# First loads reordered, the gate bias added by VectorE from a broadcast row, and the rotated key turned two tiles later

## The chip, the cores and the metric

The kernel runs on one core of one Trainium2 chip. The metric is the device time of one execution in microseconds, lower is better. Before the change three runs gave 3794.58, 3788.32 and 3795.59 us, median 3794.58 us.

## The reference, cut to what matters

Two transformer blocks run one after the other on 256 tokens of width 2048, all in float32. The change lies in the first block, ahead of its expert layer:

```python
h = rmsnorm(x, g_norm1[l])
proj = h @ w_in[l]
c_q = proj[..., :OFF_CQ]
c_kv = proj[..., OFF_CQ:OFF_CKV]
k_pe = proj[..., OFF_CKV:OFF_KPE]
z_sgu = proj[..., OFF_KPE:OFF_SGU]
gates = jax.nn.sigmoid(proj[..., OFF_SGU:] + b_gate[l])
o_a = mla_branch(c_q, c_kv, k_pe, positions, ...)   # attention; k_pe is rotated (rope) and shared by all heads
o_b = sgu_branch(z_sgu, ...)
merged = gates[..., :D_MODEL] * o_a + gates[..., D_MODEL:] * o_b
x = x + merged @ w_out[l]
```

After it come a product-key expert layer with 16384 experts (the longest part of the program), a second block with attention, a state-space scan and a gated feed-forward, which the change does not touch.

## The kernel before, in words

**Weight tiles.** Every weight matrix comes as a stream of numbered tiles of 128 partitions x 1024 float32 (512 KB). SyncE loads them into `raw`, a ring of 8, in program order. ScalarE rounds a tile to `hi` (the helper `split` of ScalarE, line 662), VectorE takes the rest, `lo = raw - hi` (line 1216), and TensorE multiplies in three passes, `xh*hi`, `xh*lo` and `xl*hi` (lines 2143 to 2145, 12 matmuls of 512 columns a tile). `hi` and `lo` are rings of 4, so ScalarE splits tile n+4 when TensorE is through with tile n. The split of n+4 stands in ScalarE's and VectorE's programs in the turn of tile n, and everything else that these engines do stands between two splits, in an order written out by hand. All waits are on semaphores.

**Start.** SyncE issues the four parts of `X` (2 MB), then eight weight tiles. GpSimd issues the constants `const`, the columns `cols`, the positions and the spatial weights `wsp`, in this order. TensorE turns `X` by transposes (`turn`, line 2176), two 128-column pieces a round, eight rounds ("h1"), of which the first two come before the first tile and the others behind tiles 0 to 5. ScalarE makes `xh` of a round (line 691), VectorE `xl` (lines 1256, 1258), and tile j needs round j. The first transpose waits for both `const` and `cols` (`small_in` at 32) and for half of `X`. The row norms of `X` come from two squares with a row sum on ScalarE (line 676), VectorE and GpSimd make the inverse root of them. The norm of a row is a factor 1/r that is multiplied in when a result leaves PSUM.

**Chunks.** A chunk is eight tiles, 512 output columns for 256 tokens, in one of two pairs of PSUM banks (`ab`), which ScalarE empties (`evac`, line 702) and gives back by `acc_free`. The order is: c_q, c_kv, the 64 columns of the key part `kpe`, then four rounds r = 0 to 3 of a gate chunk of `gm` and eight tiles of the attention's projections (parts 0 to 3 of two tiles each) for four heads, then `zv`, `zu`, the four gate chunks of `gb`, `out` and `pq`. The attention of round r-1 (`scores`, `probsT`, `values` on TensorE, `soft_in`, `soft_out` on VectorE, `probs` on ScalarE) is spread over the tiles of round r.

**Gate bias.** The result in PSUM must be r times the bias larger than the product, since the factor 1/r follows. So `gate_chunk` starts with two plain float32 matmuls of one row: the row of r (`srow`, turned by two matmuls at line 2198) times the row of the bias (`brow`, line 2278). The trace has 4 MATMUL records for the two. ScalarE's sigmoid then reads PSUM with scale 1/r and gives the banks back.

**Rotated key.** `kpe` is rotated on VectorE (`rope32`, lines 1312 to 1317) into `KPR` behind the split of tile 12 of round 0 (8 gate tiles, then 4 on), and TensorE turns it at line 2326 behind tile 9 of the round (part 0, second tile). Two memsets of `KP2` (line 1407) come before the turn is let through.

Of the kernel before, what the change touches and what calls it, by code (L numbers as in the profile page):

```python
# [12 lines left out]
ALU = mybir.AluOpType  # L13
# [4 lines left out]
P = 128  # L18
S, TT = 256, 2
D, KD = 2048, 16  # L20
CH = 512
# [23 lines left out]
ROOT1, ROOT2, STD1 = 152, 156, 160  # L45
# [55 lines left out]
MOD_TILES = (0, 4)  # L101
LNSUM = 228
# [28 lines left out]
def build(nc, A, out):  # L131
    V, SC, PE_, GP = nc.vector, nc.scalar, nc.tensor, nc.gpsimd
    ctx = ExitStack()
    with ctx:
# [37 lines left out]
        brow = at("brow", [1, 2 * CH], W0 + 73)  # L172
# [13 lines left out]
        srow = at("srow", [1, S], W0 + 85)  # L186
# [62 lines left out]
        neghalf = at("neghalf", [P, 32], W0 + 84.5)  # L249
# [65 lines left out]
        x_in = [sem(f"x_in{t}") for t in range(TT)]  # L315
        small_in, pos_in = sem("small_in"), sem("pos_in")
# [6 lines left out]
        bias_in, bias_used = [sem(f"bias_in{b}") for b in range(2)], sem("bias_used")  # L323
        kpe_T, kpe_ps, kpe_out = sem("kpe_T"), sem("kpe_ps"), sem("kpe_out")
# [3 lines left out]
        kpr_ok, row_ps, row_ok = sem("kpr_ok"), sem("row_ps"), sem("row_ok")  # L328
# [16 lines left out]
        mod2_in, mod2_used, mod2_ps = sem("mod2_in"), sem("mod2_used"), sem("mod2_ps")  # L345
# [18 lines left out]
        br_out, mod2_ok = sem("br_out"), sem("mod2_ok")  # L364
# [23 lines left out]
        def _(sp):  # L388
# [16 lines left out]
            for half in range(2):  # L405
                for t in range(TT):
                    h = slice(half * D // 2, (half + 1) * D // 2)
                    sp.dma_start(X[:, t, h], A["x"][:, t, h]).then_inc(x_in[half], 16)

            def bias(i):  # L410
                if i >= 2:
                    sp.wait_ge(bias_used, i - 1)
                sp.dma_start(brow[:, CH * (i % 2):CH * (i % 2) + CH], A["b_gate"][i:i + 1, :]).then_inc(bias_in[i % 2], 16)

            for j in range(2 * TC):
                load(A["w_in"][j], j)
# [13 lines left out]
            for j in range(8 * TC):  # L430
                load(A["w_in"][6 * TC + j], BASE["zv"] + j)
            for c in range(4):
                bias(4 + c)
                for j in range(TC):
                    load(A["w_in"][(14 + c) * TC + j], BASE["gb"] + c * TC + j)
# [49 lines left out]
        def _(pool):  # L485
            pool.dma_start(const[:], A["const"]).then_inc(small_in, 16)
            pool.dma_start(cols[:], A["cols"]).then_inc(small_in, 16)
            pool.dma_start(posi[:], A["pos"]).then_inc(pos_in, 16)
            pool.dma_start(wsp[:], A["w_spatial"]).then_inc(pos_in, 16)
            GP.memset(neghalf[:], -0.5).then_inc(pow_ok, 1)  # L490
            count = [0]
# [12 lines left out]
            pool.wait_ge(small_in, 32)  # L504
# [147 lines left out]
        def _(act):  # L652
# [51 lines left out]
            act.wait_ge(small_in, 32)  # L704
# [14 lines left out]
            act.wait_ge(trig_arg, 2)  # L719
# [3 lines left out]
            act.wait_ge(row_ps, 1)  # L723
            SC.copy(srow[:], ps[0:1, 6, 0:S]).then_inc(row_ok, 1)
            split(BASE["kpe"] + SPL)
            act.wait_ge(tile_used, BASE["kpe"] + 1)
            SC.copy(KPT[0:ROPE], ps[0:ROPE, 4, 0:S]).then_inc(kpe_T, 1)
# [29 lines left out]
            for r in range(4):  # L757
                n0, use = BASE["gm"] + (TC + 4 * TL) * r, 2 + 5 * r
                for j in range(TC):
# [9 lines left out]
                    elif j == 1:  # L769
                        act.wait_ge(kpe_ps, 1)  # L770
                        for u in range(TT):
                            SC.activation(KPE[:, u], ps[:, 5, u * ROPE:(u + 1) * ROPE], ACT.Copy,
                                          scale=stat[:, ROOT1 + 2 + u:ROOT1 + 3 + u]).then_inc(kpe_out, 1)
# [4 lines left out]
                if r == 0:  # L778
                    act.wait_ge(trig_arg, 2)
                    act.wait_ge(trig_ok, 1)  # L780
                evac(n0 + TC, use % 2, lambda t: GM[:, t, CH * r:CH * r + CH], ACT.Sigmoid, ROOT1)
                n0 += TC
                for j in range(4 * TL):
# [3 lines left out]
                    if r == 0 and j == 2:  # L787
                        act.wait_ge(row_ps, 2)
                        for b in range(2):
                            rows = slice(ROPE * b, ROPE * b + ROPE)  # L790
                            SC.copy(KP2[rows, b], ps[rows, 6, 0:S]).then_inc(row_ok, 1)
# [43 lines left out]
            for c in range(4):  # L835
# [4 lines left out]
                if c == 0:  # L840
                    act.wait_ge(ln_done, 2)
                if c >= 2:
                    act.wait_ge(merged_ok, c - 1)
                evac(BASE["gb"] + (c + 1) * TC, c % 2, lambda t: GB[:, c % 2, t], ACT.Sigmoid, ROOT1)

            def mod2_load(u):
                act.wait_ge(mod2_used, u)
                if u == 0:
                    act.wait_ge(bias_used, 8)
# [358 lines left out]
        def _(dve):  # L1208
# [53 lines left out]
            dve.wait_ge(small_in, 32)  # L1262
# [3 lines left out]
            mean_sq(2, D, 2, ROOT1)  # L1266
            for j in range(TC, TC + SPL):
                split(j)
            dve.wait_ge(rstd_ready, 1)
            V.tensor_tensor(stat[:, STD1:STD1 + 2], stat[:, ROOT1:ROOT1 + 2], stat[:, ROOT1 + 2:ROOT1 + 4], ALU.mult  # L1270
                            ).then_inc(trig_arg, 1)

            dve.wait_ge(pos_in, 32)
# [17 lines left out]
            splits(TC, TC)  # L1291

# [76 lines left out]

            split(BASE["kpe"] + SPL)  # L1370
            for r in range(4):
                n0, use = BASE["gm"] + (TC + 4 * TL) * r, 2 + 5 * r
                for j in range(TC):
# [18 lines left out]
                    if r == 1 and j in (2, 5):  # L1392
                        coefficients(j // 3)
                n0 += TC
                for j in range(4 * TL):
# [3 lines left out]
                    if r == 0 and j == 0:  # L1399
                        dve.wait_ge(kpe_out, 2)  # L1400
# [56 lines left out]
            def merge(c):  # L1457

                dve.wait_ge(acc_free[c % 2], 2 * (PB["gb"] + c // 2 + 1))
# [1401 lines left out]
```

## Time and profile before

| | |
|---|---|
| median of three runs | 3794.58 us |
| the profiled execution, its own time | 3794.6 us |
| its span, first to last instruction | 3793.0 us |
| TensorE busy | 3677.6 us, 97% |
| VectorE busy | 2672.0 us, 70% |
| ScalarE busy | 1781.7 us, 47% |
| GpSimd busy | 143.0 us, 4% |
| mean granted TensorE clock | 0.983 |
| first block up to the start of `out` | about the first 585 us |

The profile's page gives the busy time of each engine and the chain of work that ended last. A timeline lists instructions in order: start, duration, engine, line, output and inputs, and in brackets how long the engine sat idle before and who ended it. In a timeline overlapping instructions are common, the start of the next is what counts. The view of stretches gives for each the busy time of TensorE, the granted clock as a share of 2.4 GHz (1.00 or 0.50), the share in which the DMA engines were busy, and GB/s.

### The profile page before, as it was taken

How to read it: one execution, taken by the hardware profiler on the slowest of the kernel's cores; microseconds unless marked ns; L12 is line 12 of the kernel's file. 1: busy time of each engine (PE TensorE's matmuls, PEld its weight loads, DVE VectorE, ACT ScalarE, POOL GpSimd, SP SyncE). 2: the span in 40 equal slices, each digit the busy share in tenths (PEclk: the TensorE clock that was granted, in tenths of full speed). 3: DMA queues.
4: the chain of work that ended last, by engine and by line, in shares of the span. 5: the costliest groups of instructions: out<-in, count | busy, mean ns of one | idle time of the engine just before them, and what ended most of it. 6: DMA issues, size and time to landing. Idle time of an engine off the chain costs nothing.

```text
span 3793.0 us, 49880 instructions
## 1 busy us (share of the span) xinstructions
PE 3677.6 (97%) x17366; PEld 3064.2 (81%) x17366; DVE 2672.0 (70%) x3500; ACT 1781.7 (47%) x2127; POOL 143.0 (4%) x208
## 2 busy tenths in 40 slices
PE   8999999999899999999999997999999899999998
PEld 6888878888788888888888886877788688888886
DVE  4555547668797878777778886788876646666567
ACT  4554444444454444443434444556654444545553
POOL 3000000000000000000000000010000000000000
PEclk9999999999999999999999998999999899999999
DMA  6445557857558988888877874554446455555663
GB/s 220 150 145 191 186 161 271 280 176 222 178 217 307 353 296 322 296 322 298 312 266 277 282 264 153 178 162 156 157 156 197 142 169 186 189 187 184 193 186 124
DMA packets 208607, 825.92 MB, mean 218 GB/s; under 512 B 23640, under 2 KB 24152, under 8 KB 194880
## 3 DMA queue, kind: packets, MB, share of 16 engines
q1 hardware_dynamic: 175840, 638.15, 50.9%
q10 hardware_dynamic: 14400, 102.77, 7.2%
q0 software_dynamic: 18208, 82.84, 5.9%
q8 instruction: 105, 1.72, 0.2%
q14 instruction: 54, 0.44, 0.0%
HBM read 785.39 MB, written 38.27 MB: 217 GB/s over the span
## 4 chain that ended last, share of the span: by engine, by line
PE 91%; DVE 4%; ACT 3%; issue 2%; DMA 0%; POOL 0%; SPq 0%; ACTq 0%; DVEq 0%
PE ps L2143 27%; PE ps L2145 27%; PE ps L2144 27%; PE ps L2450 2%; ACT hi L662 1%; DVE lo L1216 1%; PE ps L2222 1%; PE ps L2223 1%; PE ps L2224 1%; PE ps L2583 1%; PE ps L2476 1%; PE ps L2571 1%; PE ps L2176 1%; PE ps L2237 1%; PE ps L2687 0%
## 5 line engine op out<-in xcount | busy, mean ns | idle before, releaser
L1216 DVE TENSOR_TENSOR lo<-raw,hi 128x1024 fp32r<-128x1024 f32 (+1 forms) x1217 | 1479.5, 1219 | 1013.5 <-ACT hi L662 1010.6
L662 ACT CAST hi<-raw 128x1024 fp32r<-128x1024 f32 (+1 forms) x1217 | 1274.4, 1048 | 1864.8 <-PE ps L2145 1813.7
L2143 PE MATMUL ps<-hi,xh 128*128 128x512 f32 x2880 | 1145.6, 398 | 11.0 <-DVE lo L1216 7.1
L2145 PE MATMUL ps<-hi,xl 128*128 128x512 f32 x2880 | 1128.2, 392 | 0.0
L2144 PE MATMUL ps<-lo,xh 128*128 128x512 f32 x2880 | 1127.7, 392 | 0.0
L2143 PEld LDWEIGHTS ps<-hi,xh 128*128 128x128 f32 x2880 | 545.1, 189 | 130.7 <-issue 11.6
L2145 PEld LDWEIGHTS ps<-hi,xl 128*128 128x128 f32 x2880 | 544.6, 189 | 115.7
L2144 PEld LDWEIGHTS ps<-lo,xh 128*128 128x128 f32 x2880 | 545.1, 189 | 110.5
L2143 PE MATMUL ps<-hi,Ph 128*128 128x512 f32 x1024 | 401.9, 392 | 0.0
L2145 PE MATMUL ps<-hi,Pl 128*128 128x512 f32 x1024 | 399.4, 390 | 0.0
L2144 PE MATMUL ps<-lo,Ph 128*128 128x512 f32 x1024 | 399.1, 390 | 0.0
L2145 PEld LDWEIGHTS ps<-hi,Pl 128*128 128x128 f32 x1024 | 192.6, 188 | 40.4
L2143 PEld LDWEIGHTS ps<-hi,Ph 128*128 128x128 f32 x1024 | 192.7, 188 | 39.3 <-DVE X L1670 0.2
L2144 PEld LDWEIGHTS ps<-lo,Ph 128*128 128x128 f32 x1024 | 192.7, 188 | 39.0
L1670 DVE TENSOR_TENSOR X<-X,ps 128x512 f32<-128x512 f32 x256 | 163.4, 680 | 0.0
L2143 PE MATMUL ps<-hi,Fh 128*128 128x512 f32 x352 | 140.0, 398 | 6.6 <-DVE Y L2068 5.9
L1643 DVE SCALAR_TENSOR_TENSOR macc<-mraw,stat,macc 128x2048 f32<-128x2048 f32 x60 | 140.7, 2345 | 1.4 <-DMA mraw<-in_w_mod 1.4
L2145 PE MATMUL ps<-hi,Fl 128*128 128x512 f32 x352 | 137.9, 392 | 0.0
L2144 PE MATMUL ps<-lo,Fh 128*128 128x512 f32 x352 | 137.6, 391 | 0.0
L2143 PEld LDWEIGHTS ps<-hi,Fh 128*128 128x128 f32 x352 | 66.5, 189 | 21.3 <-DVE Y L2068 7.1
L2145 PEld LDWEIGHTS ps<-hi,Fl 128*128 128x128 f32 x352 | 66.4, 189 | 14.2
L2039 DVE SCALAR_TENSOR_TENSOR cv<-ps,ccol,cv 128x255 f32<-128x255 f32 (+1 forms) x176 | 72.6, 474 | 7.4 <-ACT cv L1144 6.6
(436 smaller groups left out, 3652.7 us busy)
## 6 DMA issues: line engine op xcount, KB each, us to landing
raw<-in_peer_u SPq DMA_DIRECT2D x256, 512.0 KB, 4.8
raw<-in_peer_v SPq DMA_DIRECT2D x256, 512.0 KB, 4.6
mraw<-in_w_mod ACTq DMA_DIRECT2D x96, 1024.0 KB, 6.9
raw<-in_w_up SPq DMA_DIRECT2D x176, 512.0 KB, 3.5
raw<-in_w_in SPq DMA_DIRECT2D x144, 512.0 KB, 3.5
raw<-in_in SPq DMA_DIRECT2D x128, 512.0 KB, 3.5
raw<-in_w_down SPq DMA_DIRECT2D x88, 512.0 KB, 4.1
raw<-in_out SPq DMA_DIRECT2D x64, 512.0 KB, 4.2
```

Of the source, the lines that this page charges most:

```text
L662: SC.copy(hi[:, n0 % SPL, 0:w], raw[:, n0 % RAW, 0:w]).then_inc(hi_ready, 1)
L1216: V.tensor_tensor(lo[:, n0 % SPL, 0:w], raw[:, n0 % RAW, 0:w], hi[:, n0 % SPL, 0:w].bitcast(F32), ALU.subtract).then_inc(lo_ready, 1)
L1643: V.scalar_tensor_tensor(macc[:], mraw[:, u % 4], stat[:, 64 + u:65 + u], macc[:], ALU.mult, ALU.add).then_inc(mod_used, 1)
L1670: V.tensor_tensor(xs, xs, ps[:, 4 + 2 * (c % 2) + t], ALU.add).then_inc(v_out, 1)
L2039: ins = V.scalar_tensor_tensor(dst, src, ccol[:, q + 1 - tap:q + 2 - tap], dst, ALU.mult, ALU.add)
L2143: PE_.matmul(acc, xhi[:, k0 + k, xs], H, start=s0, stop=False)
L2144: PE_.matmul(acc, xhi[:, k0 + k, xs], L, start=False, stop=False)
L2145: mm = PE_.matmul(acc, xlo[:, k0 + k, xs], H, start=False, stop=s1)
L2176: mm = PE_.transpose(ps[:, 4 + g % 2, k * S + t * P:k * S + (t + 1) * P], src[:, t, c0:c0 + P], ident)
L2222: PE_.matmul(acc, H, xhi[:, k0 + k], start=first and k == 0 and f % 2 == 0, stop=False)
L2223: PE_.matmul(acc, H, xlo[:, k0 + k], start=False, stop=False)
L2450: mm = PE_.matmul(ps[:, 4 + b, k * P:(k + 1) * P], oh1[:, b, k], oh2[:, b, k], start=True, stop=True)
```

## The change

1. **First loads.** `X` comes in four quarters of 512 columns, each followed by weight tiles: X, w0, X, w1, w2, X, w3, w4, X, w5, w6, w7. GpSimd loads the identity (64 KB) first, then the first 304 columns of `cols` (152 KB), then the rest of `const` (497 KB) and the positions. `wsp` and the rest of `cols` follow when all eight rounds of h1 are through. The first transposes wait for the identity and the first quarter only.
2. **Squares.** The two squares over `X` and the inverse root move from between the h1 rounds to between the splits of tiles 9 and 11.
3. **Gate bias.** The bias row is loaded into all 128 partitions, `srow`, its two matmuls, and the two bias matmuls of each of the 8 gate chunks are gone. VectorE reads PSUM, multiplies by 1/r, adds the row (2 instructions a chunk, `gate_sum`) and gives the banks back, and ScalarE applies the sigmoid in place, in SBUF, in one instruction.
4. **Rotated key.** TensorE turns it behind tile 11 of round 0 instead of tile 9, and ScalarE's two copies of it move two splits on.
5. Semaphores are merged and renamed, with counts adapted.

```diff
-            for half in range(2):
-                for t in range(TT):
-                    h = slice(half * D // 2, (half + 1) * D // 2)
-                    sp.dma_start(X[:, t, h], A["x"][:, t, h]).then_inc(x_in[half], 16)
+            for q in range(4):
+                h = slice(q * CH, (q + 1) * CH)
+                sp.dma_start(X[:, :, h], A["x"][:, :, h]).then_inc(x_in[q], 16)
+                for j in ((0,), (1, 2), (3, 4), (5, 6, 7))[q]:
+                    load(A["w_in"][j], j)
...
-            pool.dma_start(const[:], A["const"]).then_inc(small_in, 16)
-            pool.dma_start(cols[:], A["cols"]).then_inc(small_in, 16)
+            pool.dma_start(const[:, 0:P], A["const"][:, 0:P]).then_inc(ident_in, 16)
+            pool.dma_start(cols[:, 0:COFF["conv"]], A["cols"][:, 0:COFF["conv"]]).then_inc(small_in, 16)
+            pool.dma_start(const[:, P:NCONST], A["const"][:, P:NCONST]).then_inc(const_in, 16)
...
             for j in range(TC):
                 turn("h1", (j,), xh, scale=lambda k: C("g1", k))
                 split(j)
-                if j in (3, 5):
-                    act.wait_ge(x_in[0], 32)
-                    act.wait_ge(x_in[1], 32)
-                    sumsq(junk[:], X[:, j // 2 - 1], stat[:, 7 + j // 2:8 + j // 2])
+            for q in range(4):
+                act.wait_ge(x_in[q], 16)
             for j in range(TC, TC + SPL):
                 split(j)
+                if j % 2:
+                    t = (j - TC) // 2
+                    sumsq(junk[:], X[:, t], stat[:, 8 + t:9 + t])
...
+            def sigmoid(dst, ab, use):
+                act.wait_ge(acc_free[ab], 2 * (use // 2 + 1))
+                SC.activation(dst, dst, ACT.Sigmoid).then_inc(sig_ok, 1)
...
-                evac(n0 + TC, use % 2, lambda t: GM[:, t, CH * r:CH * r + CH], ACT.Sigmoid, ROOT1)
+                sigmoid(GM[:, :, CH * r:CH * r + CH], use % 2, use)
...
+            def gate_sum(i, use, dst):
+                n = BASE["gm"] + (TC + 4 * TL) * i if i < 4 else BASE["gb"] + TC * (i - 4)
+                dve.wait_ge(tile_used, n + TC)
+                dve.wait_ge(bias_in[bias_slot(i)], 16 * (i // 2 + 1 if i < 6 else 1))
+                row = (brow if i < 6 else brow2)[:, i % 2]
+                for t in range(TT):
+                    V.scalar_tensor_tensor(dst[:, t], ps[:, 2 * (use % 2) + t], stat[:, ROOT1 + 2 + t:ROOT1 + 3 + t],
+                                           row, ALU.mult, ALU.add).then_inc(acc_free[use % 2], 1)
...
             def merge(c):
-                dve.wait_ge(acc_free[c % 2], 2 * (PB["gb"] + c // 2 + 1))
+                dve.wait_ge(sig_ok, 4 + c + 1)
...
-            pe.wait_ge(small_in, 32)
-            pe.wait_ge(x_in[0], 32)
+            pe.wait_ge(ident_in, 16)
+            pe.wait_ge(x_in[0], 16)
             turn("h1", (0, 1), X)
...
-            def gate_chunk(i, n, use, after=None):
+            def gate_chunk(n, use, after=None):
                 ab = use % 2
                 pe.wait_ge(acc_free[ab], 2 * (use // 2))
-                pe.wait_ge(bias_in[i % 2], 16 * (i // 2) + 16)
-                b = brow[0:1, CH * (i % 2):CH * (i % 2) + CH]
-                for t in range(TT):
-                    mm = PE_.matmul(ps[:, 2 * ab + t], srow[:, t * P:(t + 1) * P], b, start=True, stop=False)
-                mm.then_inc(bias_used, 1)
...
-                        if r == 0 and j == 1:
+                        if r == 0 and j == 3:
                             pe.wait_ge(kpr_ok, 4)
```

**ScalarE at the end of the gate chunk of round 1.** Each row is the line, the operation, output and inputs, and what it waits for. `pr` is the attention's exponential, `sc` the scores. Before:

```order
L662 CAST hi<-raw 128x512 [waits tile_used,raw_ready4]
L702 ACT_TABLE_LOAD
L702 ACTIVATE GM<-ps,stat 128x512 [waits tile_used]
L702 ACTIVATE GM<-ps,stat 128x512
L662 CAST hi<-raw 128x1024 [waits tile_used,raw_ready5]
L738 ACT_TABLE_LOAD [waits pt_ps]
L738 ACTIVATE pr,stat<-sc,stat 128x128 [waits s_max]
L740 ACTIVATE pr,stat<-sc,stat 128x256
```

The same place in the changed kernel:

```order
L680 CAST hi<-raw 128x512 [waits tile_used,raw_ready4]
L749 ACT_TABLE_LOAD
L749 ACTIVATE GM<-GM 128x2x512 [waits accB_free]
L680 CAST hi<-raw 128x1024 [waits tile_used,raw_ready5]
L760 ACT_TABLE_LOAD [waits pt_ps]
L760 ACTIVATE pr,stat<-sc,stat 128x128 [waits s_max]
L762 ACTIVATE pr,stat<-sc,stat 128x256
```

The sigmoid is one instruction now, and it waits for the banks to be given back by VectorE instead of for TensorE's last tile. Its table load still stands ahead of the wait.

**VectorE at the same place, in the changed kernel.** `sc`, the two reductions and the last `stat` are `soft_in` of a head, of which ScalarE's `pr` above is the next step.

```order
L1231 TENSOR_TENSOR lo<-raw,hi 128x512 [waits hi_ready]
L1343 SCALAR_TENSOR_TENSOR sc<-ps,const 128x384 [waits p_ready,s_ready]
L1345 TENSOR_REDUCE stat<-sc 128x1 [waits dve_step]
L1346 TENSOR_REDUCE stat<-sc 128x1
L1347 TENSOR_SCALAR stat<-stat 128x2 [waits dve_step]
L1391 SCALAR_TENSOR_TENSOR GM<-ps,stat,brow 128x512 [waits bias_in1,tile_used]
L1391 SCALAR_TENSOR_TENSOR GM<-ps,stat,brow 128x512
L1231 TENSOR_TENSOR lo<-raw,hi 128x1024 [waits hi_ready] x2
```

Before, the two `lo` rows followed the last `stat` directly, the two rows of `brow` are new, and they stand behind `soft_in`.

## Rows read from the trace of the kernel before

**Rows 1.** Timeline of TensorE, the turn of the row `srow`.

```profile
67.64 0.60 PE L2198 MATMUL ps<-const,stat 128*1 128x128 f32 x4
```

**Rows 2.** Timeline of TensorE at the start.

```profile
11.58 1.97 PE L2176 MATMUL ps<-const,X 128*128 128x128 f32 x8 [11.58 <-DMA cols<-in_cols]
17.30 0.76 PE L2143 MATMUL ps<-hi,xh 128*128 128x512 f32 x1 [3.75 <-DVE lo L1216]
```

**Rows 3.** Timeline of ScalarE at the start.

```profile
12.73 0.84 ACT L691 ACTIVATE xh<-ps,cols 128x256 fp32r<-128x256 f32 x2 [0.96 <-PE ps L2176]
14.84 1.04 ACT L662 CAST hi<-raw 128x1024 fp32r<-128x1024 f32 x1 [1.28 <-DMA raw<-in_w_in]
```

**Rows 4.** DMA: GpSimd's issue; issue to landing; X's landings; queue 0 until 6.5 us.

```profile
1.53 0.70 POOL L486 DMA_DIRECT2D const<-in_const  x1 [0.83 <-POOLq L2853]
...
const<-in_const POOLq DMA_DIRECT2D x1, 561.0 KB, 8.5
...
DMA to landing us min/median/max: 4.6/7.3/10.7
...
q0 software_dynamic: 12, 0.05, 2.5%
```

**Rows 5.** Timeline of ScalarE, a split per tile, around two chunk starts.

```profile
130.11 1.04 ACT L662 CAST hi<-raw 128x1024 fp32r<-128x1024 f32 x1 [2.37 <-PE ps L2145]
...
134.97 1.05 ACT L662 CAST hi<-raw 128x1024 fp32r<-128x1024 f32 x1 [2.35 <-PE ps L2145]
...
141.77 1.05 ACT L662 CAST hi<-raw 128x1024 fp32r<-128x1024 f32 x1 [1.67 <-PE ps L2145]
```

**Rows 6.** Stretches: start:end, us, TensorE busy (instructions), granted clock, DMA share, GB/s.

```profile
60.00:80.00 20.00, 20.00 (x103) 0.93 0.43 136
100.00:120.00 20.00, 16.72 (x108) 0.83 0.44 142
560.00:580.00 20.00, 20.00 (x80) 0.91 0.45 150
...
766.00:768.00 2.00, 0.48 (x5) 1.00 0.69 260
```

**Rows 7.** Timeline of TensorE around the turn of the rotated key.

```profile
112.19 0.69 PE L2326 MATMUL ps<-const,KPR 128*128 128x128 f32 x2 [3.28 <-DVE KP L1407]
...
117.80 0.41 PE L2222 MATMUL ps<-ckh,hi 128*128 128x256 f32 x1
```

**Rows 8.** Timeline of VectorE, ScalarE and TensorE at round 1's gate.

```profile
162.95 0.17 DVE L1333 TENSOR_SCALAR stat<-stat 128x2 f32<-128x2 f32 x1
...
163.54 1.05 ACT L662 CAST hi<-raw 128x1024 fp32r<-128x1024 f32 x1
...
166.94 0.55 PE L2246 MATMUL ps<-const,pr 128*128 128x128 f32 x3 [0.16 <-ACT pr L740]
```

**Rows 9.** Timeline behind the last gate chunk, VectorE and TensorE.

```profile
587.35 0.68 DVE L1243 TENSOR_TENSOR ml<-ps,mh 128x512 fp32r<-128x512 f32 x1
589.40 1.22 DVE L1216 TENSOR_TENSOR lo<-raw,hi 128x1024 fp32r<-128x1024 f32 x1 [1.37 <-ACT hi L662]
...
593.51 0.60 PE L2176 MATMUL ps<-const,GM 128*128 128x128 f32 x4
```

**Rows 10.** Timeline: a square, a split, inverse root, start of the angles, next splits, tile 12.

```profile
34.72 1.92 ACT L676 ACTIVATE junk<-X 128x2048 f32<-128x2048 f32 x1
...
46.04 1.05 ACT L662 CAST hi<-raw 128x1024 fp32r<-128x1024 f32 x1 [1.64 <-PE ps L2145]
...
43.05 1.53 POOL L498 TENSOR_TENSOR stat<-stat,neghalf 128x2 f32<-128x2 f32 x1 [39.07 <-DVE stat L1231]
...
48.34 0.16 DVE L1274 CAST posf<-posi 128x4 f32<-128x4 int32 x1
...
52.97 3.54 DVE L1216 TENSOR_TENSOR lo<-raw,hi 128x1024 fp32r<-128x1024 f32 x3
...
56.66 0.39 PE L2143 MATMUL ps<-hi,xh 128*128 128x512 f32 x1
```

More of the change, by code:

```diff
@@ L314, in build @@
         turn_lo = sem("turn_lo")
-        x_in = [sem(f"x_in{t}") for t in range(TT)]
-        small_in, pos_in = sem("small_in"), sem("pos_in")
+        x_in = [sem(f"x_in{q}") for q in range(4)]
+        ident_in, small_in, const_in, pos_in, late_in = (
+            sem(n) for n in ("ident_in", "small_in", "const_in", "pos_in", "late_in"))
         var_ready = sem("var_ready")
@@ L322, in build @@
         trig_arg, trig_ok = sem("trig_arg"), sem("trig_ok")
-        bias_in, bias_used = [sem(f"bias_in{b}") for b in range(2)], sem("bias_used")
-        kpe_T, kpe_ps, kpe_out = sem("kpe_T"), sem("kpe_ps"), sem("kpe_out")
+        bias_in = [sem(f"bias_in{b}") for b in range(4)]
+        sig_ok = sem("sig_ok")
         ln_in, keys_in = sem("ln_in"), sem("keys_in")
@@ L431, in _ @@
                 load(A["w_in"][6 * TC + j], BASE["zv"] + j)
+                if j >= 4 * TC and j % TC == 0:
+                    bias(j // TC)
             for c in range(4):
-                bias(4 + c)
                 for j in range(TC):
@@ L786, in _ @@
                         heads(r - 1, TC + j)
-                    if r == 0 and j == 2:
-                        act.wait_ge(row_ps, 2)
+                    if r == 0 and j == 4:
+                        act.wait_ge(rope_ps, 2)
                         for b in range(2):
                             rows = slice(ROPE * b, ROPE * b + ROPE)
-                            SC.copy(KP2[rows, b], ps[rows, 6, 0:S]).then_inc(row_ok, 1)
+                            SC.copy(KP2[rows, b], ps[rows, 6, 0:S]).then_inc(rope_out, 1)
                     if j == 1 or j == 5:
@@ L839, in _ @@
                         turn("merged", (2 * c + j - 8,), mh)
[L840 to L844, printed above, removed]
+                sigmoid(GB[:, c % 2], c % 2, 2 * PB["gb"] + c)
             def mod2_load(u):
@@ L1477, in _ @@
                         turn("merged", (2 * c + j - 8,), mh, ml)
+                if c == 0:
+                    dve.wait_ge(ln_done, 2)
+                if c >= 2:
+                    dve.wait_ge(merged_ok, c - 1)
+                gate_sum(4 + c, 2 * PB["gb"] + c, GB[:, c % 2])
             def mod2_unit(u):
@@ L2146, in tile, with chunk @@
                 mm.then_inc(tile_used, 1)
-            def chunk(n0, off, tiles, ab, pair, xhi, xlo, bias=None, meanwhile=None, row=None, before=None, after=None):
+            def chunk(n0, off, tiles, ab, pair, xhi, xlo, before=None, after=None):
                 if not isinstance(pair, int) or pair:
                     pe.wait_ge(acc_free[ab], pair * 2)
-                if bias is not None:
-                    for t in range(TT):
-                        rows = ones[0:1, :] if row is None else row[:, t * P:(t + 1) * P]
-                        mm = PE_.matmul(ps[:, 2 * ab + t], rows, bias, start=True, stop=False)
-                    if ab:
-                        mm.then_inc(bias_used, 1)
-                if meanwhile is not None:
-                    meanwhile()
                 for j in range(tiles):
@@ L2162, in chunk @@
                         before(j)
-                    tile(n0 + j, off, xhi, xlo, SL * j, 2 * ab, bias is None and j == 0, j == tiles - 1)
+                    tile(n0 + j, off, xhi, xlo, SL * j, 2 * ab, j == 0, j == tiles - 1)
                     if after is not None:
@@ L2195, in _ @@
             chunk(TC, 0, TC, 1, 0, xh, xl)
-            pe.wait_ge(trig_arg, 1)
-            for t in range(TT):
-                mm = PE_.matmul(ps[0:1, 6, t * P:(t + 1) * P], stat[:, STD1 + t:STD1 + t + 1], ident,
-                                start=True, stop=True)
-            mm.then_inc(row_ps, 1)
             n0 = BASE["kpe"]
```

115 lines of the change are left out of this document (60 added, 55 removed).

## The prediction

> **What bounds the kernel now.** I read the page's busy times first (in the table above): TensorE is busy 97% of the span, VectorE 70%, ScalarE 47%, the rest little. The chain of work that ended last says the same, 91% of it is TensorE. So a microsecond counts only when it is taken from TensorE's own program, from its clock, or from a wait of it. Next I read TensorE's waits up to 560 us, then its timeline at each of them, then the engines that it waited for. Four kinds of loss are there in the changed part. TensorE starts with its first transpose at 11.58 us, when `cols` has landed, and with its first tile at 17.30 [rows 2]. Each of the 8 gate chunks starts with small matmuls for the bias, during which the engine counts as busy and does nothing that the weights need [rows 5]. It waits 3.28 us for the rotated key [rows 7]. And the granted clock falls to half in three places [rows 6], which no list of waits shows. At full clock one tile takes TensorE 1.05 + 1.67 = 2.72 us, the period of ScalarE's splits when they follow it [rows 5].
>
> **Start.** Before, the first transpose waits for all of `const` and `cols` on GpSimd's queue. `const` was issued at 1.53 us and landed 8.5 us later, at 10.03, and by 6.5 us that queue had moved only 0.05 MB [rows 4]. The new first piece, 64 KB, is a ninth of it. It can't land before about 6.5 us, nor later than 10.03. I take 7.7: some 0.4 us for its bytes behind 6.3, and 1 us from last byte to landing, close to the lower end because it is small. The first quarter of X, as large as each part of X before and in the same place, lands 4.6 us after its issue at about 1.0, at 5.6 [rows 4], and doesn't gate. From the first transpose to `xh` it is 12.73 - 11.58 = 1.15 us, the two `xh` take some 0.75, then the split of tile 0 starts, and tile 0 follows 17.30 - 14.84 = 2.46 later [rows 2, 3]. Before, this split also waited 1.28 us for tile 0's weights, which came fifth on SyncE's queue [rows 3]. Now they come second, and by half the bytes they are there before 9.6. So tile 0 starts at 7.7 + 1.15 + 0.75 + 2.46 = 12.1, a gain of 5.2 us. The bounds: a piece that lands at 10.03 gives 2.9, one that lands with X at 5.6 gives 7.3. The later rounds need a quarter of X and two weight tiles each, about 1.5 MB per 6.5 us of TensorE's time, which the queues moved faster than before. I cost the spread at nothing. What covers it is that each tile of h1 takes 3.2 us, and if the cover were gone a late quarter would stall TensorE by its own lateness.
>
> The Trainium skill, page "DMA: Bandwidth & Descriptors", section "Anatomy of one DMA", puts a GpSimd-issued transfer at about 2.0 us plus its bytes at 436 GB/s. By that, as an estimate from the page, the 64 KB would land at 3.7 us, X would gate the start, and this term would be 7.3 instead of 5.2. The row for `const` does not agree with it: 8.5 us for 561 KB, where the page gives 3.3.
>
> **Squares and angles.** The squares go from the h1 rounds, where they delayed two rounds by a tenth or two each, to behind splits 9 and 11. The split of tile 11 started at 46.04 [rows 10] (TensorE frees its slot then), the second square follows and ends at 46.04 + 1.05 + 1.92 + 0.2 = 49.2. VectorE's mean, GpSimd's inverse root of 1.53 and two handovers make 51.1. The angles' chain took 52.97 - 48.34 = 4.63, so VectorE's split of tile 12 comes at 55.7 and ends at 57.0, where TensorE wants it at 56.66 [rows 10]. This is 0.4 us late. With 0.2 won back in the rounds the term is -0.2, bounds +0.3 and -1.5. What is queued behind ScalarE's wait for the root is c_q's evacuation and splits that have slack.
>
> **Gate bias, what goes.** The turn of `srow` goes, four records from 67.64 on for some 0.5 us [rows 1]. At the start of round 1's gate chunk ScalarE's splits are 134.97 - 130.11 = 4.86 apart, of which 2.72 is the tile [rows 5]. The bias costs 2.14 us of TensorE's time in each of 8 chunks: 17.1 us. Nothing hides it now, since TensorE is the engine that does it.
>
> **Clock.** From 60 to 80 us the granted clock was 0.93, from 560 to 580 it was 0.91 [rows 6]. (1 - 0.93) x 20 + (1 - 0.91) x 20 = 1.4 + 1.8 = 3.2 us of loss. Both falls, to 1.2 GHz, came right behind a pair of bias matmuls, which itself followed other weak work (the 64-column key part, a transpose). The other six pairs brought none. I take 3.0 back, bounds 0 and 3.2.
>
> **Rotated key.** TensorE was through with tile 9 at 112.19 - 3.28 = 108.9 and began tile 12 at 117.80, 8.9 us later, for a wait, the turn, and two half-width tiles at half clock (the 0.83 from 100 to 120) [rows 6, 7]. Now the two tiles come first, 1.4 us each at full clock, until 111.8. VectorE has the key ready 0.7 us later than before, since the split ahead of it waits for the sigmoid (below), at 112.9. TensorE waits 1.1 us instead, turns, and begins tile 12 at 113.3: gain 4.5 us, bounds 2.5 (the clock falls as before for some of it) and 5.2.
>
> **Gate bias, what comes.** Two VectorE instructions a chunk, PSUM to SBUF, 128x512. The nearest is `ml<-ps,mh` of this shape, 0.68 us [rows 9], two overlapping make 1.3. Then the sigmoid, one 128x1024 instruction in SBUF; the nearest is the split, 1.05 [rows 8]. VectorE has 30% to spare, so its 10 us cost nothing in themselves, and the banks come free in time. What costs is the order on ScalarE. In rounds 1 to 3 the gate stands ahead of the attention's exponential, and there TensorE already waits 0.16 us for `pr` [rows 8]. VectorE is in `soft_in` until 163.1, the sums end at 164.4, the sigmoid at 165.4. Its table load lies ahead of the wait (the rows of ScalarE's order above) and is hidden. So the next split starts at 165.35 instead of 163.54 [rows 8], and all behind it, table load, `pr`, TensorE's transpose of `pr`, is 1.8 late. Three rounds make -5.4 us. The bounds are 1.4 and 2.4 a round, from the sigmoid 0.4 shorter or 0.6 longer. Round 0 has no such chain.
>
> Behind the last gate chunk `merge(3)` must wait for the sigmoid. `ml` of the last turn starts at 587.35 and ends at 588.0 [rows 9], the sums at 589.3, the sigmoid at 590.4, the next `hi` at 591.35. Then `lo` starts at 591.4 instead of 589.40, and with three VectorE instructions of 1.2 (`lo`, and `merge`'s two) the merged rows are there at 595.0 and TensorE at 595.1, where it turned them at 593.51 [rows 9]: -1.6 us, bounds -0.8 and -2.5. In the other gb chunks the merge comes three to five tiles later and is covered.
>
> **Sum** against the profiled execution, 3794.6 us with a span of 3793.0, the same as the median: 5.2 - 0.2 + 0.5 + 17.1 + 3.0 + 4.5 - 5.4 - 1.6 = 23.1, so 3771.5 us.
>
> **Rivals.**
> 1. *The first piece lands early* (the page's rule above, or simply a shorter queue). Tile 0 starts at 10.0, the sum is 25.2, 3769.4 us. For it: it is a ninth of `const`. Against it: nothing at all came over that queue in the first 6 us. Chance 0.12.
> 2. *The longer waits take the clock.* TensorE's waits for `pr` grow to 2.0 us in three rounds, and after the wait of 3.28 for the key the clock went to half [rows 6, 7]. A fall costs about 1.6 to 1.8 each, as from 560 to 580. Three of them, and one in the new 1.1 us wait, make 6.5, so 3778. Against it: at 766 us TensorE was busy 0.48 of 2 us and the clock stayed at 1.00 [rows 6]. Chance 0.15.
> 3. *The gain doesn't come, within 0.2%.* The bias matmuls would have to cover something that TensorE then waits for, such as the sigmoid's delay reaching the splits in all eight chunks. The splits run four tiles ahead, 4 x 2.72 = 10.9 us, and the delayed one is ready some 7 us after the chunk's end. If ScalarE or VectorE were 4 us slower than I think, each chunk would lose what goes beyond, and 2 us in each of eight eat 16 of the 23 us: 3787. Chance 0.06.
> 4. *Slower.* The same mechanism at its full price, the new hand-over from VectorE to ScalarE holding all splits: it decides from about 3 us of stall a chunk on beyond my terms, 8 x 3 = 24 us, and at 4 us gives 3803.6 us. The slack of 4 us ahead of it would have to be gone too, so the sigmoid would have to come 8 us late. No row shows such an instruction. Chance 0.04.
>
> **How the numbers follow.** My forecast has 0.63, and rivals 1 to 4 the rest. The likeliest one's own range adds the bounds in part, 3767 to 3776. The range for 8 in 10 takes in rivals 1 and 2 and small shifts of the clock in later stages, whose falls of some 1.7 us each may come or go when the program is 23 us earlier: 3764 to 3780. About 0.2%, 7.6 us, is what a measurement of this kernel can tell from no change. Faster has 0.63 + 0.12 + 0.15 = 0.90, the same 0.06, slower 0.04.
>
> **What would show it.** The first transpose at 7.7 and tile 0 at 12.1. No plain float32 matmuls at the chunk starts, splits 2.72 apart there. Clock at 1.00 between 70 and 80 and, in the shifted place, behind the last gate chunk. A wait of about 1.1 us before the rotated key's turn, no half clock behind it. Three waits for `pr` of about 2 us, and one of 1.6 before the first merged turn in `out`. The prediction is wrong if those three waits bring half clock, if the identity lands at 10 us, or if ScalarE's splits starve TensorE at the gates.

## The result and the profile after

The changed kernel takes 3775.46 us in the median of 5 runs (3767.91 to 3776.25), the kernel before took 3794.65 us on the same chip (3788.32 to 3797.09). The ratio is 0.995, with an interval of 0.9939 to 0.996: 19.2 us faster, where 23.1 were forecast. One of 17 later executions of the kernel before took 7521.67 us, about twice the others, and no comparison below uses it. The profiled execution has a span of 3774.0 us. TensorE stays the bound, busy for 97% of it:

```profile
span 3774.0 us, 49824 instructions
PE 3658.2 (97%) x17330; PEld 3058.0 (81%) x17330; DVE 2683.6 (71%) x3515; ACT 1779.1 (47%) x2118; POOL 144.9 (4%) x210
```

TensorE's busy time fell by 3677.6 - 3658.2 = 19.4 us with 36 matmul records less, and VectorE's rose by 11.6 us, nearly all of it the sums of the bias. The list of TensorE's waits until 620 us (in total, times, longest) is the first thing to read, since the prediction rests on four of them, those for `const`, `pr`, `GM` and `KP`:

```profile
PE ps L2266 <- ACT pr L762: 7.9, 5, 2.0
PE ps L2201 <- DMA const<-in_const: 7.1, 1, 7.1
PE ps L2176 <- DVE lo L1231: 3.1, 2, 2.9
PE ps L2201 <- DVE GM L1491: 1.4, 1, 1.4
PE ps L2201 <- DVE CKV L1411: 1.3, 1, 1.3
PE ps L2340 <- DVE KP L1435: 1.1, 1, 1.1
```

The first wait of 11.58 us [rows 2] is now 7.1, that for the rotated key is 1.1 instead of 3.28 [rows 7], that for `pr` has grown from 2.3 to 7.9 in all, three of its five pieces 2.0 us long, and one of 1.4 us for the merged rows is new. The timeline at the start, with the rows that gate tile 0:

```profile
7.06 1.97 PE L2201 MATMUL ps<-const,X 128*128 128x128 f32 x8 [7.06 <-DMA const<-in_const]
8.63 0.21 ACT L723 ACTIVATE stat<-cols 128x16 f32<-128x16 f32 x1 [6.35 <-DMA cols<-in_cols]
9.46 1.04 ACT L680 CAST hi<-raw 128x1024 fp32r<-128x1024 f32 x1
11.91 0.77 PE L2176 MATMUL ps<-hi,xh 128*128 128x512 f32 x1 [2.88 <-DVE lo L1231]
```

The identity has landed at 7.06 us, the piece of `cols` at 8.63, and tile 0 starts at 11.91 instead of 17.30 [rows 2]. At round 1's gate the timeline reads, in the order of what waits for what:

```profile
146.76 0.17 DVE L1347 TENSOR_SCALAR stat<-stat 128x2 f32<-128x2 f32 x1
146.84 1.41 DVE L1391 SCALAR_TENSOR_TENSOR GM<-ps,stat,brow 128x512 f32<-128x512 f32 x2
148.28 1.06 ACT L749 ACTIVATE GM<-GM 128x1024 f32<-128x1024 f32 x1 [2.10 <-DVE GM L1391]
150.30 1.28 ACT L760 ACT_TABLE_LOAD   x1
151.99 0.49 ACT L762 ACTIVATE pr<-sc,stat 128x256 f32<-128x256 f32 x1
152.63 0.55 PE L2266 MATMUL ps<-const,pr 128*128 128x128 f32 x3 [2.04 <-ACT pr L762]
```

The maximum of the attention's scores is there at 146.93. ScalarE could go on to its exponential then, but it first stands idle until the sums are done (2.10 us in all), does the sigmoid, a split and a table load, and TensorE stands for 2.04 us. Before, the same chain left it 0.16 us of wait [rows 8]. The granted clock, by stretches:

```profile
60.00:80.00 20.00, 20.00 (x113) 1.00 0.43 130
100.00:120.00 20.00, 18.85 (x120) 1.00 0.55 175
240.00:260.00 20.00, 18.16 (x113) 1.00 0.42 132
260.00:280.00 20.00, 19.80 (x127) 0.91 0.48 146
560.00:580.00 20.00, 18.57 (x89) 1.00 0.77 267
```

The three falls of before in this part, to 1.2 GHz, are gone [rows 6]. A new one has come between 260 and 280 us, right behind the third of the 2.0 us waits, which ends at 260.20.

**Where the 19 us are.** Both programs run the same matmuls in nearly the same order, so the start of one and the same matmul in either trace shows how far ahead the changed kernel is there. "Ahead" is the start before less the start after, and the last column what was added since the line above:

```
start before   ahead   since the line above
   17.30        5.38   first loads, tile 0
   66.18        5.00   first two tiles, -0.5 between 21 and 24 us; the rest +0.1
   70.06        5.69   turn of srow gone: +0.7
   76.02        7.80   bias matmuls, round 0: +2.1
   92.93        9.31   no half clock from 77 us on: +1.5
  118.01       13.99   rotated key: +4.7
  150.09       16.19   bias, round 1: +2.2
  183.06       14.32   wait for pr: -1.9
  189.07       16.46   bias, round 2: +2.1
  222.00       14.55   wait for pr: -1.9
  243.06       16.66   bias, round 3: +2.1
  290.02       13.09   wait for pr -1.9, and the new half clock -1.7
  556.09       19.44   bias, three gb chunks: +6.3
  580.07       23.19   bias +2.1, no half clock near 562 us: +1.6
  597.04       21.57   merge(3): -1.6
 1940.20       21.64   nothing in 1300 us
 1960.21       20.36   a half clock of 1920 to 1940 us is longer: -1.3
 3780.14       18.98   small shifts of the clock in later stages: -1.4
```

So 21.6 us are won in the part that was changed, and 2.6 of them are lost again in stages that weren't. The same working for e5 below, a second execution of the changed kernel, gives 21.5 us at 597.04 and 1.2 lost behind it, so more than half of the 2.6 is this one execution's.

### The profile page after: what moved, and what is told of

It is laid out like the page before. It is cut to its first block, busy times and chain, and to the rows that moved or that the text cites. A ratio compares the mean times of both kernels' runs of the same rounds, so it can differ in the third digit from the quotient of the medians.

```text
span 3774.0 us, 49824 instructions
## 1 busy us (share of the span) xinstructions
PE 3658.2 (97%) x17330; PEld 3058.0 (81%) x17330; DVE 2683.6 (71%) x3515; ACT 1779.1 (47%) x2118; POOL 144.9 (4%) x210
## 4 chain that ended last, share of the span: by engine, by line
PE 90%; DVE 4%; ACT 3%; issue 2%; DMA 0%; POOL 0%; ACTq 0%; DVEq 0%; POOLq 0%
PE ps L2176 27%; PE ps L2178 27%; PE ps L2177 27%; PE ps L2464 2%; ACT hi L680 1%; DVE lo L1231 1%; PE ps L2242 1%; PE ps L2244 1%; PE ps L2243 1%; PE ps L2597 1%; PE ps L2490 1%; PE ps L2585 1%; PE ps L2257 1%; PE ps L2201 1%; PE ps L2701 0%
## 5 line engine op out<-in xcount | busy, mean ns | idle before, releaser
L2176 PEld LDWEIGHTS ps<-hi,Fh 128*128 128x128 f32 x352 | 66.8, 190 | 21.5 <-DVE Y L2101 7.2
```

Of the source, the lines that this page charges most:

```text
L2176: PE_.matmul(acc, xhi[:, k0 + k, xs], H, start=s0, stop=False)
```

## The experiments

The profile's ledger adds up, but an addition is not yet a cause. The theory is that the terms are independent, and that the two losses (the order on ScalarE in rounds 1 to 3, and `merge(3)`) are waits that a different order removes. The rivals stand in each expectation. All comparisons are with the kernel before on the same chip. The times of one and the same kernel lie 4 to 11 us apart, so a ratio's interval is 6 to 12 us wide, and for a single term the trace is the sharper instrument: "ahead" below is always against the trace of the kernel before, at the same matmuls as in the table above.

### e1: the bias matmuls put back

```diff
                 pe.wait_ge(acc_free[ab], 2 * (use // 2))
+                for t in range(TT):
+                    PE_.matmul(ps[:, 2 * ab + t], ident[0:1, :], X[0:1, t, 0:CH], start=True, stop=True)
                 for j in range(TC):
```

> The changed kernel with two small float32 matmuls of the bias's shape (1x128 by 1x512) put back at the start of each of the 8 gate chunks, their result overwritten by the tile's first matmul, so the output stays the reference's; VectorE's sums and ScalarE's sigmoid stay as changed. Theory (additive terms): they cost 2.1 us a chunk whatever else was changed, 8 x 2.14 = 17.1 us, so about 3792.6 us, and up to 3 more if the half clock between 60 and 80 us and near 560 us comes back with them (3795.5). Rival (the matmuls covered waits, and the gain came elsewhere): under 10 us more, below 3785.

Measured: 3793.95 us (11 runs), ratio 1.0006, interval 0.9997 to 1.0015. The whole gain is gone. In the ledger "ahead" stands at 5.95 at 70.06 and at 5.94 at 76.02, so the pair takes back all of its 2.1 us, and the same at the other seven chunks; at 597.04 only 0.18 of the 21.57 us are left. That is more than the 17.1 us of the matmuls. The gains that e1 still has (the start, the key) are eaten by its waits and by the clock. What it lost beyond the 17.1 is clock, the stretches of e1 with a fall behind such a pair being these:

```profile
500.00:520.00 20.00, 20.00 (x78) 0.91 0.48 152
560.00:580.00 20.00, 20.00 (x84) 0.91 0.48 152
120.00:140.00 20.00, 19.23 (x84) 0.91 0.39 126
```

Each 0.91 is 1.8 us. The fall near 560 us came back as forecast, that between 60 and 80 did not, and two came where before had none. So a pair can bring a fall, but which one does differs from trace to trace; e7 below says the same. The rival (the matmuls covered something) is out.

### e2 and e7: the rotated key's turn, early in the changed kernel, late in the kernel before

```diff
-                        if r == 0 and j == 3:
+                        if r == 0 and j == 1:
                             pe.wait_ge(kpr_ok, 4)
...
-                    if r == 0 and j == 4:
+                    if r == 0 and j == 2:
                         act.wait_ge(rope_ps, 2)
```

> The changed kernel with the rotated key's turn two tiles earlier again, behind tile 9; all else as changed. Theory (the wait and the half clock behind it were the price): the wait before the turn is 3 to 4 us again, the clock is at half behind it, and the time grows by 4.3 to 5, to 3780 us. Rival (only the wait moved, the clock falls whatever stands there or not at all): the wait grows by about 2.7 us with no half clock, 3778.2 us; or the place is free: within 1 us of 3775.5.

Measured: 3775.24 us (5 runs, 3771.86 to 3778.89), ratio 0.9952, interval 0.9938 to 0.9965: by the times, no loss. By the trace, a loss where it was expected. The wait and the stretches behind it, in e2's profile:

```profile
PE ps L2340 <- DVE KP L1435: 4.0, 1, 4.0
102.00:104.00 2.00, 1.04 (x5) 0.61 0.25 100
104.00:106.00 2.00, 2.00 (x12) 0.54 0.27 76
```

The wait is 4.0 us and the clock is at its lower level behind it. "Ahead" is 10.52 at 118.01, where the changed kernel has 13.99 with a slower start of its own; over the stretch from 92.93 it rises from 9.98 to 10.52, by 0.5 against 4.7. These 4.2 us are not given back by 597.04, where e2 has 16.75 and the changed kernel 21.57. The profiled execution was also the slowest of its five, 3778.89. The times alone could not say, so the reverse was tried: the kernel before with nothing but this turn moved (j == 1 to j == 3 on TensorE, j == 2 to j == 4 on ScalarE).

> The kernel before with nothing changed but the rotated key's turn, two tiles later. Theory (what e2 showed in its profile, 5.4 us at this place, holds; its equal median was spread of the runs): the wait of 3.28 us falls to 0.4 or less, since VectorE's split ahead waits for no sigmoid sum here, the half clock behind it goes (3.4 to 6.8 us long, 1.7 to 3.4 us of loss), gain 4.5 to 6 us, 3788.5 us. Rival (what e2's times say: the place costs nothing in the end, since a half-clock stretch saved here comes back at a later wait): within 2 us of before.

Measured: 3789.88 us (12 runs), before 3792.08, ratio 0.9993, interval 0.9984 to 1.0001. The wait in e7's profile:

```profile
PE ps L2326 <- DVE KP L1407: 0.4, 1, 0.4
```

"Ahead" rises from 1.00 at 92.93 to 6.39 at 118.01, +5.4 us, as the theory has it. Then half-clock stretches come where the trace of before has none, behind round 1's start and near 532 us, and it is 4.78 at 597.04, 0.65 at 1060 and 5.91 at 3780:

```profile
120.00:140.00 20.00, 19.54 (x77) 0.91 0.36 111
520.00:540.00 20.00, 20.00 (x81) 0.91 0.47 139
```

Both come behind a pair of bias matmuls, which this kernel still has, and the two falls that before had behind other pairs (60 to 80 and 560 to 580) did not come. Over the three traces with all eight pairs (before, e1, e7) 7 of 24 pairs were followed by a fall, two or three in each. So the local price of the early turn is 4.2 and 5.4 us in two traces of two different kernels, the timed gain is 2 to 3 us with an interval that just reaches zero, and part of such a gain can be taken back by the clock elsewhere. The rival is half right: not that the place is free, but that a fall saved in one place may be paid in another.

### e3: ScalarE's sigmoid behind the exponential

```diff
-                sigmoid(GM[:, :, CH * r:CH * r + CH], use % 2, use)
                 n0 += TC
                 for j in range(4 * TL):
                     split(n0 + SPL + j)
                     if r:
                         heads(r - 1, TC + j)
+                    if j == 0:
+                        sigmoid(GM[:, :, CH * r:CH * r + CH], use % 2, use)
```

> The changed kernel with ScalarE's sigmoid of the gates of rounds 0 to 3 one place later in its program: behind the next split and the attention's exponential instead of ahead of them. Theory (the order on ScalarE makes the three waits for the exponential): TensorE's waits for pr of 2.0 us in rounds 1 to 3 fall to under 0.3, 1.85 x 3 = 5.6 us, and with the wait of round 3 the half clock between 260 and 280 us goes too, 1.7 us: 3768.2 us. The rotated key may be ready 0.7 us sooner: 3767.5. Rival (VectorE is what delays: the two sums of 1.3 us stand ahead of its split and of the maximum): the waits keep 1.2 us or more each and the gain is at most 2.5 us, 3773.

Measured: 3762.56 us (5 runs, 3758.78 to 3765.03), ratio 0.9919, interval 0.9906 to 0.9933: below every run of the changed kernel, and more than was expected. VectorE's sums stay where they were, so its rival falls. In e3's timeline at the same gate the exponential comes first, the sigmoid fits behind it, and TensorE's turn of `pr` waits for nothing:

```profile
144.23 1.05 ACT L680 CAST hi<-raw 128x1024 fp32r<-128x1024 f32 x1 [2.25 <-PE ps L2245]
145.58 0.50 ACT L762 ACTIVATE pr<-sc,stat 128x256 f32<-128x256 f32 x1
146.19 1.28 ACT L749 ACT_TABLE_LOAD   x1
147.48 1.06 ACT L749 ACTIVATE GM<-GM 128x1024 f32<-128x1024 f32 x1
147.52 0.49 PE L2267 MATMUL ps<-const,pr 128*128 128x128 f32 x3
```

"Ahead" goes from 19.10 at 150.09 to 19.05 at 183.06, where the changed kernel lost 1.9, and likewise in rounds 2 and 3. No half clock is recorded anywhere in the first 620 us. The waits until 620 us:

```profile
PE ps L2267 <- ACT pr L762: 2.0, 3, 1.0
PE ps L2202 <- DVE GM L1492: 1.4, 1, 1.4
```

The wait for the rotated key isn't in the list any more: VectorE's `lo` ahead of it waits for ScalarE's `hi`, which no longer stands behind the sigmoid. At 597.04 e3 is 32.4 us ahead of before, 10.8 more than the changed kernel: 6.1 in the three rounds, 1.7 of clock, 1.2 at the key, and 1.6 at the start, which is not the edit's (see the first microseconds, at the end). So the edit is worth 9 us by the trace. Between the two profiled executions lie 15.9 us, and 5.2 of them come behind 600 us, where e3 changes nothing (it gains 2.6 there, the changed kernel loses 2.6). The medians lie 12.9 apart, with an unknown share of such shifts in it.

### e4 and e8: what gates the start

In e4 ScalarE issues the identity and the first part of `cols` on its own queue; in e8 `const` comes whole again ahead of `cols`, with x in quarters as changed.

```diff
# e4
-            pool.dma_start(const[:, 0:P], A["const"][:, 0:P]).then_inc(ident_in, 16)
-            pool.dma_start(cols[:, 0:COFF["conv"]], A["cols"][:, 0:COFF["conv"]]).then_inc(small_in, 16)
+            act.dma_start(const[:, 0:P], A["const"][:, 0:P]).then_inc(ident_in, 16)
+            act.dma_start(cols[:, 0:COFF["conv"]], A["cols"][:, 0:COFF["conv"]]).then_inc(small_in, 16)
...
# e8
-            pool.dma_start(const[:, 0:P], A["const"][:, 0:P]).then_inc(ident_in, 16)
+            pool.dma_start(const[:], A["const"]).then_inc(ident_in, 16)
...
-            pool.dma_start(const[:, P:NCONST], A["const"][:, P:NCONST]).then_inc(const_in, 16)
```

> The changed kernel with the identity and the first part of cols issued by ScalarE on its own queue instead of by GpSimd. Theory (GpSimd's queue is what makes the first pieces land at 7.06 and 8.63 us): they land at 5 to 6.5 us, the first quarter of X (5.5 us after its issue at 1.0) then sets the start, the first transpose begins at about 6.6 and tile 0 at about 10.8 instead of 11.91, gain 1.1 us. Rival (nothing lands before 6.5 us on any queue, they share the engines with X and the weights): first transpose at 7 us or later, tile 0 at 11.9 or later, no gain.

> The changed kernel with const loaded whole again ahead of cols on GpSimd's queue; x in quarters and all else as changed. Theory (the start goes by when the identity and cols land): const lands at 9.5 to 10 us and cols behind it at about 10.5, so the first transpose begins at about 9.8, tile 0 at about 14.0 instead of 11.91, 2.1 us later. Rival (x in quarters among the weights is what made the start earlier): tile 0 within 0.7 us of 11.91, since its split waits for the weights anyway.

Measured: e4 3771.76 us (4 runs), ratio 0.9947, interval 0.9932 to 0.9963; e8 3772.63 us (4 runs), ratio 0.9948, interval 0.9933 to 0.9962. Neither is told from the changed kernel by its time. The starts in the traces, first e4's with its two issues on ScalarE's queue (KB each, us from issue to landing), then e8's:

```profile
6.98 1.94 PE L2201 MATMUL ps<-const,X 128*128 128x128 f32 x8 [6.98 <-DMA X<-in_x]
9.89 1.04 ACT L678 CAST hi<-raw 128x1024 fp32r<-128x1024 f32 x1 [0.94 <-DMA raw<-in_w_in]
12.34 0.77 PE L2176 MATMUL ps<-hi,xh 128*128 128x512 f32 x1 [3.42 <-DVE lo L1231]
const<-in_const ACTq DMA_DIRECT2D x1, 64.0 KB, 1.9
cols<-in_cols ACTq DMA_DIRECT2D x1, 152.0 KB, 5.8
```

```profile
9.57 1.97 PE L2200 MATMUL ps<-const,X 128*128 128x128 f32 x8 [9.57 <-DMA const<-in_const]
13.90 0.77 PE L2175 MATMUL ps<-hi,xh 128*128 128x512 f32 x1 [2.36 <-DVE lo L1230]
```

In e4 the identity landed 1.9 us after its issue, at about 2.9, where GpSimd's queue took 5.5 us for the same 64 KB. So the identity does come sooner, and the rival's reason is wrong, but its outcome is right: x is there only at 6.98, tile 0's weights only at 9.89, and tile 0 starts at 12.34, 0.4 us later than in the changed kernel. In e8 tile 0 is at 13.90, 2.0 us later than in the changed kernel, as its theory had it. Of the 5.4 us at the start, `const` in pieces gives 2.0; the other 3.4 are left to x in quarters, tile 0's weights early and the shorter first part of `cols`, which no run took apart.

### e5: the changed kernel once more

> The changed kernel once more, as it is, as the reference for the others on this chip. Theory (half-clock stretches of 3.4 us, each 1.7 us of loss, come and go from run to run and make most of the spread of single times): the median is within 3 us of 3775.5, and the list of half-clock stretches behind 600 us differs from the first profile's in one or more. Rival (the stretches are fixed by the program): the same list as before, to the microsecond.

Measured: 3774.31 us (5 runs, 3770.79 to 3775.25), ratio 0.9949, interval 0.9936 to 0.9962. The waits until 620 us are the same to 0.1 us. The clock is not: this execution has a second fall behind a wait for `pr`, from 140 to 160 us, while behind 600 us the falls stand in the same places, and only the last two, behind 3750 us, are shorter. So the theory was half right: falls that come and go lie in the changed part, behind the waits. The later ones stayed, as the rival has it; this execution arrives there within 0.3 us of the first one. The two stretches of e5 with a fall behind a wait for `pr`:

```profile
140.00:160.00 20.00, 17.96 (x124) 0.91 0.44 137
260.00:280.00 20.00, 19.65 (x127) 0.91 0.45 147
```

Its start is 1.4 us better with the same waits, see below on the first microseconds.

### e6: both waits removed

e3, and the last two turns of merged rounds one tile later, on all three engines (TensorE's part is shown):

```diff
-                    if c == 0 and j in (2, 3):
+                    if c == 0 and j in (3, 4):
                         pe.wait_ge(merged_ok, 4)
-                        turn("merged", (4 + j,), GM)
+                        turn("merged", (3 + j,), GM)
```

> The kernel of e3 (sigmoid one place later), and the last two turns of merged rounds behind tiles 3 and 4 of out instead of 2 and 3. Theory (the merged rows are 1.43 us late, a tile takes 2.72 us): the wait before that turn goes, 1.4 us less than e3, about 3761 us, 0.991 of before. Rival (the turn's result is then late for tile 6 of out): TensorE waits for the turned rows instead, no gain over e3.

Measured: 3759.95 us (5 runs, 3758.92 to 3763.12), ratio 0.9916, interval 0.9903 to 0.9928. It beats both kernels: 32.1 us faster than before by the medians, 14.4 than the changed kernel on the same chip. The wait for `GM` is gone from its list, and none for the turned rows has come:

```profile
PE ps L2267 <- ACT pr L762: 2.0, 3, 1.0
PE ps L2202 <- DVE CKV L1412: 1.3, 1, 1.3
PE ps L2364 <- DVE ZU L1316: 0.2, 1, 0.2
```

From 580 to 760 us e6 stays 32.5 us ahead of before, where e3 drops from 34.0 to 32.3. That the merge's share of 1.7 us is real is shown by the trace; the times of e3 and e6 overlap and don't tell it. e6 has no half clock in the first 620 us either. Of its lead at the end, 35.7 us, 3.2 were added behind 600 us and are no part of the edit.

## Why the prediction was right, step by step

The forecast was 3771.5 us within 3764 to 3780, and 3775.46 was measured. Its terms against the ledger:

- **Start, +5.2.** Tile 0 came at 11.91 for a forecast 12.1, +5.4. The first transpose came at 7.06, not 7.7: the 64 KB took 5.5 us from issue to landing. They began to move at 4.6 us, not 6.3, took 1.9 us, not 0.4, and landed 0.5 us behind the last byte, not 1. But `cols`, which the prediction left out of the chain, landed at 8.63: `xh` started at 8.75 and not 1.15 us behind the transpose, at 8.21, so the two errors nearly cancelled, which was luck. Even where the identity did land at 2.9 us (e4) tile 0 came no sooner, because x (forecast for 5.6, there at 6.98 in e4) and the weights were next. Rival 1 is out on both counts. By the Trainium skill, page "DMA: Bandwidth & Descriptors", section "Anatomy of one DMA", 64 KB on GpSimd's path take 2.2 us, as an estimate from its figures. The row of 5.5 us does not agree with it. e8 shows that only 2.0 us of this term are the division of `const`.
- **Squares and angles, -0.2.** They cost nothing. The ledger's -0.4 until 66 us all comes between 21 and 24 us, in the slow pace of the first matmuls (see the end), where e5 with the same squares gains 1.0 in the same two tiles; from 24 to 66 us it rises by 0.1. VectorE's split of tile 12 was forecast 0.4 us too late. It started at 49.87 and took 1.2, and TensorE came to that tile at 51.7 without a wait:

```profile
49.87 4.68 DVE L1231 TENSOR_TENSOR lo<-raw,hi 128x1024 fp32r<-128x1024 f32 x4
```

  That the number fits its bounds is chance.
- **Gate bias, +0.5 and +17.1.** +0.7 for the turn of `srow`, and 2.1 to 2.2 at each of eight chunks, 17.0. e1 shows it from the other side.
- **Clock, +3.0.** +1.5 and +1.6. But e1 and e7 showed that the falls aren't tied to these two pairs: with the pairs in place, e1 had one of the two and two others, e7 neither of the two and two others. Two or three of the eight pairs bring one, so the size was right, and the attribution to what went before in these two places was wrong.
- **Rotated key, +4.5.** +4.7, with the wait of 1.1 us that was forecast (1.15 in the timeline) and no half clock. e2 and e7 give 4.2 and 5.4 for it.
- **Gate bias, what comes, -5.4.** Three waits of 2.04 us, -1.9 each, -5.6. e3 shows that the order on ScalarE was the cause and that VectorE's sums themselves cost nothing: with them in place and the sigmoid behind the exponential, the loss is gone.
- **merge(3), -1.6.** -1.6, as a wait of 1.43 us. e6 removes it.

With one fall, -1.7, these make 21.6 us where 23.1 were summed. The prediction named its own sign of being wrong, "if those three waits bring half clock", and this sign came in part. What failed is a step that was kept apart from the sum: rival 2, "the longer waits take the clock", had a chance of 0.15 as a whole and a price of 1.6 to 1.8 us a fall, and one of its four falls came, 1.7 us in the first trace, two in the trace of e5. Over the six traces with 2.0 us waits for `pr` (the changed kernel, e1, e2, e4, e5 and e8) the three waits were followed at once by a fall in one, one, two, two, two and two cases, 10 of 18. At the same places without a wait of that length, in e3, e6, e7 and before, there was none in 12. So the waits bring the falls, in a bit over half of the cases, and the right entry in the sum was some 3 x 0.55 x 1.7 = 2.8 us, a term and not a rival. The row that was held against it, no fall at 766 us, was itself one outcome of two: that place is a single wait of 2.45 us, and in five of the ten traces a fall does follow it. The rest of the miss, 2.6 us in this trace and 1.2 in e5's, lies behind 600 us, where nothing but names and counts of semaphores was changed. The prediction named it for its range ("may come or go") and gave it no sign. Over the nine traces held against the one of before, the lead changes there by between -2.6 and +3.2 us. What makes these later falls move was not settled. At the work that the changed kernel does around 1740 us it has one, as have before, e1, e2 and e5; e3, e4, e6, e7 and e8 have none:

```profile
1740.00:1760.00 20.00, 20.00 (x80) 0.87 0.92 364
1920.00:1940.00 20.00, 19.31 (x94) 0.83 0.65 239
```

```profile
1740.00:1760.00 20.00, 20.00 (x92) 1.00 1.01 406
1920.00:1940.00 20.00, 19.32 (x91) 0.91 0.67 236
```

The first pair is the changed kernel's, the second e4's. The instructions there are the same and TensorE is as busy in either. The moment of arrival alone doesn't explain it in a simple way: e5 arrives 0.3 us behind the changed kernel's first execution and has the same falls, e4 only 0.5 us behind e5 and has the first not at all and the second half as long. No run shifted the arrival alone, and the cause stays open.

## What to carry to other kernels

When work moves from one engine to a chain of two, the price is not in their busy time but in what stands behind the second engine's new wait: put the waiting instruction behind the one that the bound engine needs next (here one place in ScalarE's program was worth 9 us, half of what the whole change had brought). Follow the same matmul through both traces and note how far ahead it is; a ledger of this kind separates terms of 2 us where the times of one kernel are spread over 4 to 11. Close it where the changed part ends: the stages that nobody touched moved by -2.6 to +3.2 us from trace to trace, and a median has that in it. Count falls of the clock as a term with a chance behind every wait of about 2 us.

## What the runs showed of the hardware

- A 64 KB piece issued by GpSimd at 1.52 us landed 5.5 us later, the same piece issued by ScalarE at 1.00 us landed 1.9 us later; `cols`, 152 KB, issued next on the same queues, took 6.4 and 5.8 us. So over ScalarE's queue the first piece was there 4.1 us sooner, and the second, with x and the weights on their way, 1.4.
- The first matmuls ran at half pace though the granted clock of the stretch from 10 to 20 us reads 1.00. In the changed kernel's profile this lasted for all of tile 0 and into tile 1, in that of e5, the same kernel, it ended in the middle of tile 0. The rows are e5's; the spacing of the starts goes from 0.43 to 0.23 us:

```profile
13.77 0.63 PE L2177 MATMUL ps<-lo,xh 128*128 128x512 f32 x1
14.20 0.63 PE L2178 MATMUL ps<-hi,xl 128*128 128x512 f32 x1
15.05 0.39 PE L2177 MATMUL ps<-lo,xh 128*128 128x512 f32 x1
15.28 0.39 PE L2178 MATMUL ps<-hi,xl 128*128 128x512 f32 x1
```

  It makes 1.4 us of difference between two executions of one program (6.43 against 5.00 us ahead at 66.18), as much as the smaller terms of this study, and e3 had the luck of it too (6.65), e6 not (5.35).
- Two executions of the same program agree in every wait to 0.1 us and differ in which of these waits the clock falls behind. Over the ten traces none of the 32 waits of TensorE of 1.0 to 1.5 us in the first 620 us was followed at once by a fall, 10 of the 18 of 2.04 us were, and both of 3.3 and 4.0 us were. Further on a wait of 2.45 us (ending at 767.52 us in before) was followed by a fall in 5 of the 10 traces, and one of 2.0 us ahead of a tile (ending at 984.09 us in before) in all 10. So the length of a wait alone doesn't decide.
